# A fused two-block transformer kernel: order of normalise and split in the first mixer, own banks and another order for the MLA latents

## What is computed

```
# first mixer: eight heads of 64, q and k normalised per head
qa, ka, va, qb, kb, vb, qi, ki, wi, g = split(rmsnorm(h) @ w_in)
qa = rmsnorm(qa per head); ka, qb, kb likewise
# latent attention
lat = rmsnorm(h) @ w_dkv
c_q  = rmsnorm(lat[:384]);  c_kv = rmsnorm(lat[384:640]);  k_pe = lat[640:704]   # one key for all heads
q = c_q @ w_uq;  kv = c_kv @ w_ukv;  q_pe, k_pe = rotate(.., cos, sin)
```

## Time and profile before

| what | us |
|---|---|
| median of 3 runs | 1326.08 (1325.56 to 1326.24) |
| the profiled execution | 1325.89 |
| its span, first to last instruction | 1324.1 |
| TensorE matmuls busy | 1273.8 (96%) |
| VectorE busy | 760.2 (57%) |
| ScalarE busy | 648.3 (49%) |
| mean granted TensorE clock | 0.992 |

### The profile page before, as it was taken

The page is one execution under the profiler, slowest core; times in us unless marked ns, Lnnn a source line. Parts: engine busy times, 40 slices in busy tenths (PEclk is TensorE's granted clock), DMA queues, the critical chain, the costliest instruction groups (busy, mean ns, idle before and its releaser), DMA issues.

```text
span 1324.1 us, 16795 instructions
## 1 busy us (share of the span) xinstructions
PE 1273.8 (96%) x6754; PEld 1088.0 (82%) x6754; DVE 760.2 (57%) x1083; ACT 648.3 (49%) x828; POOL 11.9 (1%) x16
## 2 busy tenths in 40 slices
PE   6999998999999999998999999999999989999996
PEld 5888887888888888887888799999787867889895
DVE  5554549787676555548655475554644545754544
ACT  5444436454455444436844464443646635643432
POOL 0000000001000000000000000000000000000000
PEclk9999999999999999999999999999999999999998
DMA  6855546553434655545523265553464322655530
GB/s 233 303 189 187 184 151 216 186 175 130 174 130 136 223 189 189 191 128 182 189 98 112 80 239 183 186 191 133 175 233 162 122 70 90 210 205 186 183 124 32
DMA packets 38685, 221.72 MB, mean 167 GB/s; under 512 B 4533, under 2 KB 4549, under 8 KB 23120
## 3 DMA queue, kind: packets, MB, share of 16 engines
q1 hardware_dynamic: 36256, 214.26, 46.3%
q0 software_dynamic: 912, 3.75, 0.9%
q10 hardware_dynamic: 1440, 2.64, 0.7%
HBM read 219.55 MB, written 1.07 MB: 167 GB/s over the span
## 4 chain that ended last, share of the span: by engine, by line
PE 86%; DVE 7%; ACT 5%; issue 2%; DMA 0%; DVEq 0%; SPq 0%; ACTq 0%
PE ps L377 22%; PE ps L379 22%; PE ps L378 22%; PE ps L572 4%; PE ps L574 4%; PE ps L573 4%; DVE wlo L357 3%; PE ps L1268 2%; PE ps L1288 2%; ACT whi L349 2%; PE ps L899 1%; PE ps L409 1%; PE ps L1277 1%; ACT xt_h L419 1%; PE ps L605 1%
## 5 line engine op out<-in xcount | busy, mean ns | idle before, releaser
L357 DVE TENSOR_TENSOR wlo<-w_raw,whi 128x2048 fp32r<-128x2048 f32 (+4 forms) x245 | 469.4, 1924 | 394.7 <-ACT whi L349 394.3
L349 ACT ACTIVATE whi<-w_raw 128x2048 fp32r<-128x2048 f32 (+4 forms) x245 | 394.5, 1616 | 433.6 <-PE ps L379 329.7
L377 PE MATMUL ps<-whi,xt_h 128*128 128x512 f32 (+3 forms) x784 | 309.7, 395 | 9.1 <-DVE wlo L357 4.0
L379 PE MATMUL ps<-whi,xt_l 128*128 128x512 f32 (+3 forms) x784 | 303.7, 387 | 0.0
L378 PE MATMUL ps<-wlo,xt_h 128*128 128x512 f32 (+3 forms) x784 | 303.2, 387 | 0.0
L377 PE MATMUL ps<-whi,ot_h 128*128 128x512 f32 x594 | 237.2, 399 | 5.1 <-ACT nat L944 2.7
L379 PE MATMUL ps<-whi,ot_l 128*128 128x512 f32 x594 | 233.5, 393 | 0.0
L378 PE MATMUL ps<-wlo,ot_h 128*128 128x512 f32 x594 | 233.2, 393 | 0.0
L377 PEld LDWEIGHTS ps<-whi,xt_h 128*128 128x128 f32 x784 | 148.2, 189 | 43.5 <-ACT whi L349 7.8
L379 PEld LDWEIGHTS ps<-whi,xt_l 128*128 128x128 f32 x784 | 148.0, 189 | 29.8
L378 PEld LDWEIGHTS ps<-wlo,xt_h 128*128 128x128 f32 x784 | 148.2, 189 | 27.3
(11 more groups left out here) (184 smaller groups left out, 861.6 us busy)
## 6 DMA issues: line engine op xcount, KB each, us to landing
w_raw<-ffn_mid SPq DMA_DIRECT2D x80, 768.0 KB, 4.3
w_raw<-mlp_mid SPq DMA_DIRECT2D x56, 1024.0 KB, 4.9
w_raw<-w_qkv SPq DMA_DIRECT2D x12, 1024.0 KB, 4.9
w_raw<-w_sb_qkv SPq DMA_DIRECT2D x12, 1024.0 KB, 5.0
w_raw<-w_xkv SPq DMA_DIRECT2D x8, 1024.0 KB, 4.9
w_raw<-ffn_first SPq DMA_DIRECT2D x8, 512.0 KB, 4.9
w_raw<-w_gate_b SPq DMA_DIRECT2D x4, 1024.0 KB, 4.8
w_raw<-w_gate_a SPq DMA_DIRECT2D x4, 1024.0 KB, 4.9
```

The costliest lines, as they stand in the source:

```text
L349: nc.scalar.activation(whi[:, s, 0:tiles * width], w_raw[:, s, 0:tiles * width], ACT.Copy).then_inc(w_hi, 1)
L357: nc.vector.tensor_tensor(wlo[:, s, 0:tiles * width], w_raw[:, s, 0:tiles * width], whi[:, s, 0:tiles * width].bitcast(F32), ALU.subtract) ...
L377: nc.tensor.matmul(acc, hi, whi[:, s, c], start=start, stop=False)
L379: return nc.tensor.matmul(acc, lo, whi[:, s, c], start=False, stop=stop)
```

## The change

Five things:

1. In `vector`, a qk unit's `normalise` stands ahead of `next_lo` of its last chunk, no longer behind it.
2. The "dkv" unit is multiplied into `bankD[1]` and not into `bankA`. It doesn't wait for the copy of the first latent any more, and the first up unit waits for the first latent's copy in place of the second's. The turn of the memory waits for the second latent's copy (new wait).
3. `mla_down` gets orders of its own for ScalarE and VectorE (`latents_scalar`, `latents_vector`), with copies, squares and the taking ahead of splits.
4. The taking of the second latent's transposes moves behind the copy of the first up unit (ScalarE).
5. The shared key of both tiles is rotated at once (`rotate_shared`): 8 VectorE instructions of 2 x 32 columns in place of 16 of 32.

```diff
+            def bank_of(self, unit, t):
+                return bankD[1][t] if unit.kind == "dkv" else bankA[t]
@@ multiply
-                            if part and part[0] == unit.ks[0] and unit.u > 0:
+                            if part and part[0] == unit.ks[0] and unit.u > 0 and unit.kind != "dkv":
                                 pe.wait_ge(self.evac, NT * (unit.u - 1) + t + 1)
                             if part and part[0] == unit.ks[0] and unit.u == 0 and self.before:
-                                pe.wait_ge(self.before.evac, NT * (len(self.before.units) - 1) + t + 1)
+                                pe.wait_ge(self.before.evac, NT * (len(self.before.units) - 2) + t + 1)
...
-                                last = mm3(bankA[t][:, 0:unit.width], self.stat_h[:, k, t * P:(t + 1) * P],
+                                last = mm3(self.bank_of(unit, t)[:, 0:unit.width], self.stat_h[:, k, t * P:(t + 1) * P],
...
+            def latents_scalar(self, act):
+                first, second = self.units
+                self.copy_out(act, first)
+                next_hi(act, first.n[0][0])
+                self.latent_squares(act, first)
+                self.take(act, first)
+                next_hi(act, first.n[1][0])
+                self.copy_out(act, second)
+                self.latent_squares(act, second)
+                next_hi(act, second.n[0][0])
+                next_hi(act, second.n[1][0])
+
+            def latents_vector(self, dve):
+                first, second = self.units
+                next_lo(dve, first.n[0][0])
+                self.lower(dve, first)
+                self.root(dve, first)
+                next_lo(dve, first.n[1][0])
+                self.rotate_shared(dve, second)
+                next_lo(dve, second.n[0][0])
+                next_lo(dve, second.n[1][0])
+                self.root(dve, second)
+                self.lower(dve, second)
@@ scalar
+                if self.hand_on:
+                    return self.latents_scalar(act)
...
-                    if before is not None and self.hand_on:
-                        self.take(act, before)
                     self.copy_out(act, unit)
+                    if self.before and unit.u == 0:
+                        self.before.take(act, self.before.units[-1])
...
+            def rotate_shared(self, dve, unit):
+                dve.wait_ge(tables.trig, 1)
+                dve.wait_ge(self.evac, NT * (unit.u + 1))
+                x1, x2 = (nat[:, unit.u % 2, :, KL + a * HALF:KL + (a + 1) * HALF] for a in range(2))
+                cos, sin = trig[:, 0], trig[:, 1]
...
+                nc.vector.tensor_tensor(part[0], x1, cos, ALU.mult)
+                nc.vector.tensor_tensor(part[1], x2, sin, ALU.mult)
+                nc.vector.tensor_tensor(part[2], x1, sin, ALU.mult)
+                own(dve, dve_own, nc.vector.tensor_tensor(part[3], x2, cos, ALU.mult))
+                for c in range(2):
+                    nc.vector.tensor_tensor(lg[:, :, c * ROPE:c * ROPE + HALF], part[0], part[1], ALU.subtract)
+                    last = nc.vector.tensor_tensor(lg[:, :, c * ROPE + HALF:(c + 1) * ROPE], part[2], part[3], ALU.add)
+                last.then_inc(self.made, NT)
@@ vector
-                before = None
+                if self.hand_on:
+                    return self.latents_vector(dve)
...
+                    if unit.kind == "qk":
+                        self.normalise(dve, unit)
                     if not (self.select and unit is self.units[-1]):
                         next_lo(dve, unit.n[-1][0])
-                    if unit.kind == "qk":
-                        self.normalise(dve, unit)
...
         def mem_norm(i):
-            return Norm(f"mem{i}", [(xt_lo, 4 * NORM[f"mem{i}"])])
+            return Norm(f"mem{i}", [(xt_lo, 4 * NORM[f"mem{i}"])] + [mla_down.evac_ready] * (i == 0))
```

More of the change, by code:

```diff
@@ L943, in copy_out @@
                     else:
-                        nc.scalar.activation(self.nat_of(unit, t)[:, 0:w], bankA[t][:, 0:w], ACT.Copy,
+                        nc.scalar.activation(self.nat_of(unit, t)[:, 0:w], self.bank_of(unit, t)[:, 0:w], ACT.Copy,
                                              scale=row).then_inc(self.evac, 1)
@@ L997, in scalar @@
                         next_hi(act, unit.n[-1][0])
-                    if unit.kind in ("latent", "dkv"):
-                        self.latent_squares(act, unit)
-                    if before is not None and not self.hand_on:
+                    if before is not None:
                         self.take(act, before)
@@ L1029, in rotate @@
                 dve.wait_ge(tables.trig, 1)
-                heads = 1 if unit.kind == "dkv" else H2
-                at = KL if unit.kind == "dkv" else 0
+                w = H2 * HALF
                 for t in range(NT):
@@ L1035, in rotate @@
                         dve.wait_ge(self.made, NT * unit.made + t)
[L1036 to L1040, removed]
+                    x1, x2 = (self.nat_of(unit, t)[:, a * w:(a + 1) * w]
+                              .rearrange("p (h d) -> p h d", h=H2) for a in range(2))
+                    cos, sin = (trig[:, a, t].unsqueeze(1).to_broadcast([P, H2, HALF]) for a in range(2))
+                    part = [pt[:, a // 2, (a % 2) * 256:(a % 2) * 256 + w].rearrange("p (h d) -> p h d", h=H2)
                             for a in range(4)]
@@ L1045, in rotate @@
                     own(dve, dve_own, nc.vector.tensor_tensor(part[3], x2, cos, ALU.mult))
[L1046 to L1051, removed]
+                    to = lg[:, t, 0:H2 * ROPE].rearrange("p (h d) -> p h d", h=H2)
+                    nc.vector.tensor_tensor(to[:, :, 0:HALF], part[0], part[1], ALU.subtract)
+                    nc.vector.tensor_tensor(to[:, :, HALF:ROPE], part[2], part[3], ALU.add).then_inc(self.made, 1)
+            def rotate_shared(self, dve, unit):
[3 more added lines that the diff above has]
+                cos, sin = trig[:, 0], trig[:, 1]
+                part = [pt[:, a // 2, (a % 2) * 256:(a % 2) * 256 + NT * HALF].rearrange("p (t d) -> p t d", t=NT)
+                        for a in range(4)]
+                nc.vector.tensor_tensor(part[0], x1, cos, ALU.mult)
[6 more added lines that the diff above has]
+                last.then_inc(self.made, NT)
             def root(self, dve, unit):
@@ L1080, in vector @@
                         self.squares(dve, unit)
-                    if before is not None and before.kind in ("latent", "dkv"):
-                        self.lower(dve, before)
-                    if unit.kind in ("dkv", "pe"):
+                    if unit.kind == "pe":
                         self.rotate(dve, unit)
@@ L1086, in vector @@
                         self.aside.vector(dve)
+                    if unit.kind == "qk":
+                        self.normalise(dve, unit)
                     if not (self.select and unit is self.units[-1]):
                         next_lo(dve, unit.n[-1][0])
-                    if unit.kind == "qk":
-                        self.normalise(dve, unit)
-                    if unit.kind == "latent":
-                        self.root(dve, unit)
                     if self.select and unit.u == 4:
@@ L1097, in vector @@
                         self.select.take_eight(dve)
-                    before = unit
-                if before.kind in ("latent", "dkv"):
-                    self.root(dve, before)
-                    self.lower(dve, before)
             def sync(self, sp):
```

## The result

The changed kernel takes 1313.58 us (median of 4 runs, 1312.95 to 1314.68); the kernel before, run beside it, 1325.82 (4 runs, 1322.65 to 1326.24). The ratio is 0.9917 with an interval of 0.9904 to 0.993: faster by 0.8%. The forecast was 1313.8.

A forecast was written before the change was run, and what follows sets the result against it. TensorE is busy nearly all of the span, so only its waits and slow stretches can be won. Gains of 3.9 + 8.3 = 12.2 us off 1325.89 give 1313.7, forecast as 1313.8; range 1311.3 to 1317.8.

The forecast's parts named there:

- Site A: First mixer's projections: swapping normalise and split cuts the 3.15 us wait to 0.94 and avoids half speed; 3.9 us gained.
- Site B: Latents and up-projection: shorter waits and full clock give 6.9 + 1.6 - 0.2 = 8.3 us.
- Site B's first wait: At 610.00, before the second latent: VectorE's split replaces ScalarE's copy as what TensorE waits for; only 0.5 us gained.
- The second wait: At 619.74, 1.64 us for the first latents' low parts: goes in full, with cover 1.1 us.
- The third wait: At 629.10, 2.71 us: copying the up-projection's first unit before the taking lets the next unit start at 622.2.
- the rotated key: Needed for the second latent's turn at 621.5: rotation takes 1.1 us, ready at 621.4, no cover.
- 0.2 charged behind it: After the memory's norm: VectorE reaches the query's rotation some 0.5 us later against TensorE; 0.2 us charged.
- The clock at site B: Half speed behind the waits at 619.74 and 629.10 goes: 18 matmuls take 4.22 us, not 5.83 and 5.80.
- The stretch at 1067: Half speed after the stick-breaking attention's 4.74 us wait: a shift could cost up to 1.7 less, hardly more; taken as 0.
- Rival 1: Transposes count like idling, so the clock falls at A and once in B, 1.7 each: 1315.5 to 1317.2; chance 0.12.
- Rival 2: Latents' chain on VectorE and ScalarE 2 us late, perhaps a clock fall of 1.7: 1315.8 to 1317.5; chance 0.13.
- Rivals 3 and 4: 3: gain taken back later, 1320 to 1326, chance 0.04; 4: clock stays low through site B, 1333, chance 0.02.

The follow-up runs named there:

- before_again: The kernel before, unchanged, profiled a second time: that execution took 1322.72 us.
- b_only: Changed kernel with the swap of normalise and split undone: 1317.96 us, ratio 0.9962 to the kernel before.
- banks_only: Kernel before with only the second latent's own banks, all orders as before: 1325.57 us against 1322.79, ratio 1.0015.
- one_bank: Changed kernel with the second latent back in the first one's banks, with its waits for the copies: 1313.62 us.
- rotate_tiles: Changed kernel with the shared key rotated tile by tile, sixteen instructions: 1313.94 us.
- pad1: Changed kernel with one extra unused square (128x512) ahead of the first unit's normalise: 1313.55 us.
- take_first: Changed kernel with ScalarE taking the second latent's transposes ahead of the first up unit's copy again: 1317.47 us.
- a_only: Kernel before with only the swap of normalise and split in the first mixer: 1321.54 us against 1325.23, ratio 0.9979.
- both_early: Changed kernel with the first w_dkv chunk split early and the stick-breaking mixer's first unit copied ahead of a split: 1310.62 us, ratio 0.9897 to before.

## Why the prediction was right, and where it wasn't

**Site A, 3.9 us: right, 3.75.** The residual wait was 0.94 as worked out, the clock stayed up. In all four traces with 3.1 us of wait (before, before_again, b_only, banks_only) the half-speed stretch is there: 219.01 to 219.38 against 215.6. The swap's other side, a split 1.3 us later, cost nothing that any part shows.

**Site B's first wait, 0.5 of 1.46 gained: right, 0.4.** VectorE's split took the place of the copy, with 1.06 us left. The prediction gave this gain to the bank of its own, and this step failed in its reason: one_bank has the same wait without it. The order of ScalarE did it, since the copy then comes before VectorE's split.

**The second wait gone with 1.1 us of cover: right,** the low parts ended at 611.7 and were wanted at 612.8. The profile of the changed kernel shows it; no run takes that move away alone.

**The third wait and the rotated key: right.** Rotation took 1.3 us and not 1.1, ready at 616.8 against 616.9: there was just no cover, as the prediction said, and in rotate_tiles, where rotating took 0.7 us longer, 0.79 was lost. The second unit began 4.86 us after the first; the prediction had 4.9.

**0.2 charged behind it: not seen.** The query's transposes took 1.30 us, and 1.32 before. Site B came to 8.54 in place of 8.3.

**The clock at site B, counted at 1.6 behind each of two waits: right for the profile that was read, wrong as a rule.** In some half of the executions of the kernel before the clock stays up behind both, and site B is then worth 5.3 us (255.05 - 249.80) and not 8.5. "Three of the four lie where the change works, so each of those waits costs itself and then some 1.6 us" held in every trace at A only. The forecast of the changed kernel's own time didn't suffer, since the sum was made against an execution with all the stretches; against the 18 lower times of the kernel before the gain is about 9 us, against the 21 upper ones about 12.

**The stretch at 1067, "can cost up to 1.7 less, hardly more": wrong in the second half.** The prediction reckoned with a stretch of one length, 3.4 us, all of it already on matmuls; in nine of the 14 profiles it is 6.8 us long. Over the traces the last part takes 256.85 to 258.26; in the changed kernel's first profile it cost 0.58 more than in that of before, with half speed from 1052 to 1058.8. The start of the kernel gave 0.77 back, as the pace there rose earlier, which the prediction doesn't have. That the two nearly cancel is luck, worth about 0.2 of the agreement.

**Rival 1, transposes don't hold the clock up:** fell. The turn of the memory and of a unit, 24 transposes in a row that take 2.5 us from the first's start to the next matmul's (2.9 by the modelled ends), has no fall behind it in any of the 14 profiles, while the waits of 2.15 and 2.38 us were followed by one. At A, the 0.94 us wait and its transposes, 2.0 to 2.2 in all, left the clock up in all eight profiles that have them. Behind pad1's 1.53 us wait there are 1.25 us of transposes, 2.8 in all, and the clock is at 1.00 from 224.5 to 228.0; this one alone would not decide, as the clock stayed up behind 2.71 us of waiting too. The rule of the Trainium skill that it went with (TensorE: Matmul & The Clock Gate, Part 4: PE-mode transpose) is not borne out for these float32 transposes. **Rival 2, a late chain:** the lack of cover was real, the lateness not. **Rivals 3 and 4:** no wait behind 660 grew; no half speed at site B in any trace of the changed order (take_first, with its wait of 2.71 us back, has one stretch).

## What to carry to other kernels

When an engine that splits or copies ahead sits on the path only by its order, price its steps one by one and find which instruction the waiting engine needs first; moving two copies ahead of eight small instructions gave half of site B, while a bank more gave nothing. Take one part away at a time before crediting it: the part named first in a change may be idle. A wait behind which the clock falls costs its own length and 1.6 us more: here the clock fell behind none up to 1.53 us, behind 1.80 and 2.71 in some executions, and behind the others from 2.15 on in each profile. So lengthening one wait by what another gives up (banks_only, 1.80 to 2.38) can lose; and take two or three profiles of the kernel before, as one may stand for only half of its executions.

## What the runs showed of the hardware

- Behind waits of TensorE of 0.94, 1.06, 1.31, 1.46 and 1.53 us no trace here has a half-speed stretch (1.53: one trace). Behind 2.15 and 2.38 (one trace each) and 3.13 to 3.16 us (four) each trace has one, of about 3.4 us. By the 18 matmuls of 5.83 and 5.80 us against 4.22 it costs 1.6; it costs less where it begins ahead of the restart (before_again at A).
- Behind 1.80 and 2.71 us in one execution of the kernel before it is there, and in another it isn't, nor in a_only with the same waits. Behind the 2.71 of take_first and banks_only it is there. What decides it, within an execution, was not tried; the times fall in two groups 3.3 us apart, so the two stretches seem to come together.
- Behind the 4.73 us wait the stretch lasts 3.4 us in five of the profiles (before, banks_only, rotate_tiles, both_early, pad1: last part 256.85 to 257.08) and 6.8 in the nine others (257.62 to 258.26).
- Float32 transposes of 128x128 ran at full speed and held it: 24 in a row, 2.5 us, with the clock at 1.00 and no fall behind, in all 14 profiles.
- The column of the granted clock doesn't show everything: it reads 1.00 from 14 to 15.5 us, where matmuls of 512 columns begin 0.43 us apart in each trace, behind waits of 7.3 and 4.0 us; 0.23 is their distance later.
- VectorE's instruction on 128x64 takes 0.22 us, and on 128x32 0.18: twice the columns for a fifth more.
